# Three partial products of split fp32 weights replaced by one plain fp32 product, in a two-layer encoder on one core

## The chip, the core and the metric

The kernel runs on one NeuronCore of a Trainium2 chip. TensorE multiplies, VectorE, ScalarE and GpSimd work element by element, and SyncE issues most DMAs. The metric is the device time of one execution in microseconds (us); less is better. The change may touch anything inside the kernel, as long as the output is the reference's.

## What is computed

Two layers of an encoder over 256 tokens of 1024 float32 values. Cut to what matters:

```
for layer in range(2):
    hn   = rmsnorm(h, mix_norm_pre[layer])
    proj = hn @ w_in[layer]                  # (256,1024) @ (1024,2048): u, q, k, v of 512 columns each
    y    = concat(pool_mixer(u),             # window means of 2, 4, 8, 16 tokens, each @ a 128x128 matrix
                  neighbourhood_attention(q, k, v))   # 16 heads of 32, 4x64 token grid, 4x16 window
    h    = h + rmsnorm(y @ w_out[layer])     # (256,1024) @ (1024,1024)
    hn   = rmsnorm(h, ffn_norm_pre[layer])
    if layer == 0: f = (silu(hn @ w_gate) * (hn @ w_up)) @ w_down     # dense, inner width 4096
    else:          f = top-2-of-8 experts, the same form, inner width 3584 each
    h    = h + rmsnorm(f)
```

All weights are float32: 12 MB per mixing part (w_in and w_out), 48 MB of dense weights, and 336 MB of expert weights, which are all read once.

## The kernel before

**Stages.** The program is straight-line code for each engine, with semaphores. In order: mixing of layer 0, dense layer, mixing of layer 1, routing, eight expert items, a tail. Between the stages stands a norm (`norm_pair`), whose result is transposed on TensorE (`transposes`, L768) into the tokens `hT`. TensorE's order is written out by hand in each function; nothing is planned by the program but the order of experts.

**Weights of the mixing and dense stages.** SyncE loads them in pieces of 2 MB (a "load", `load` at L456) into a ring of `RING` = 3 buffers. A load has two halves. Before TensorE can use a half, ScalarE rounds it to fp32r (`split_to` at L1177, the ACTIVATE at L1189 that writes `w_hi`), and VectorE writes the rest, `w_lo` = weight - `w_hi` (L1424; in the attention stretch in two parts, L1435). The tokens have the same two parts, `hT_hi` and `hT_lo`, and so have the other left operands (`yaT`, `ypT`, `dhid`). `w_hi` and `w_lo` hold `STAGE` = 3 halves. A load goes on once VectorE has split the one that stood in its buffer.

**A product.** One product is a 128x128 stationary block times 256 or 512 columns. `product` (L728) makes it of three fp32r matmuls:

```python
mm(dst, still[0], moving[0], start=start, stop=False)
mm(dst, still[0], moving[1], start=False, stop=False)
return mm(dst, still[1], moving[0], start=False, stop=stop)
```

The first half of a stage goes through `open_half` (L739), which does the same three in another order (L750, L759). The projection of one mixing stage has 8 halves (`fill(f, part)`, two parts of 8 products of 256 columns), 128 products in all; its output projection has 32 products of 512 columns. The dense layer has 512 products of 256 columns (gate, up) and 128 of 512 columns (down).

Other matmuls (the experts, attention, pooling, the transposes and `keep_busy`) take plain float32 operands. A plain float32 matmul of the program stands as two MATMUL records in the trace; an fp32r matmul stands as one.

**Attention.** It goes in 8 groups g. For each: `scores(g)` on TensorE (L818), `add_bias(g)` on VectorE (L1571 and the minimum at L1573), four exponentials on ScalarE (`exps`, L1292), `normalise(g)` on VectorE (a reciprocal at L1579 and four scalings at L1581), `turn(g)` on TensorE (transposes, L827), a copy on ScalarE (`probs_out`, L1300), and after two groups `values` on TensorE (L844). All groups share the bank `pa` for scores. Before, TensorE's loop is this, and VectorE's loop body is `add_bias(g)`, a half split of weights, `normalise(g)`:

```python
for g in range(GROUPS):
    if g < 7:
        scores(g + 1)
    fill(4 + g // 2, g % 2)
    if g == 7:
        values(2)
    turn(g)
    if g in (3, 4):
        values(g - 3)
```

GpSimd writes the attention bias (`build_bias`, L579) and the window means of pooling (`window_delta`, L387); one of the four means is VectorE's. The four products of the pooling matrices are plain float32 (L926), 256 columns each.

**Experts.** The 192 expert weight "units" of 1792 KB go to 12 slots that lie over the buffers of the earlier stages. `load_unit` (L493) waits for whatever held the slot; the first 12 units are loaded during the mixing of layer 1 and the routing, the others when TensorE is done with a slot. TensorE computes in 32-column strips, four side by side (L1077 for gate and up, L1086 for down). The items take 3, 2, 3, 3, 2, 3, 3 and 2 token groups.

Of the kernel before, what the change touches and what calls it, by code (L numbers as in the profile page):

```python
# [6 lines left out]
ACT = mybir.ActivationFunctionType  # L7
AX = mybir.AxisListType
F32 = mybir.dt.float32
F32R = mybir.dt.float32r  # L10
I32 = mybir.dt.int32

P = 128
D = 1024
# [39 lines left out]
RING = 3  # L54
STAGE = 3
# [3 lines left out]
assert 2 * MOE0 % STAGE == 0  # L59
UNIT = FE  # L60
SLOTS = 12
H_SLOT = 10
# [12 lines left out]
FILL_ENGINE = (0, 1, 0, 0, 0, 1, 0, 1)  # L75
FILLS = (FILL_ENGINE.count(0), FILL_ENGINE.count(1))

# [6 lines left out]
SLOT_OF = [n % SLOTS for n in range(N_UNITS - 2)] + [SLOTS - 1, 0]  # L84
# [25 lines left out]
def hybrid_encoder(nc, x, mix_pre, mix_post, ffn_pre, ffn_post, w_in, pool_w, pool_scale, rpb,  # L110
                   w_out, d_gate, d_up, d_down, router, e_gate, e_up, e_down, consts, out):
    with ExitStack() as ctx:
# [19 lines left out]
        addr = {}  # L132
        bias = sb("bias", [P, HEADS * 2 * ROWS * WIN])
# [5 lines left out]
        w_hi = sb("w_hi", [P, STAGE, 8 * C2], F32R)  # L139
        w_lo = sb("w_lo", [P, STAGE, 8 * C2], F32R)  # L140
        uT = sb("uT", [P, 4, S + 2 * POOL_PAD])
        pt23 = sb("pt23", [P, 2, D])
        h = sb("h", [P, NT, D])
        gpost = sb("gpost", [P, D])
        win_b = sb("win_b", [P, S + 2 * POOL_PAD])
# [3 lines left out]
        assert addr["bias"] + 4 * UNIT * H_SLOT <= addr["h"] and addr["win_b"] <= addr["bias"] + 4 * UNIT * (H_SLOT + 1)  # L149
        sb("spare", [P, (addr["bias"] + 4 * UNIT * SLOTS - plan_top[0]) // 4])  # L150
        hs = sb("hs", [P, NT, D])
        hT_hi = sb("hT_hi", [P, DT, S], F32R)
        hT_lo = sb("hT_lo", [P, DT, S], F32R)
# [6 lines left out]
        ypT_lo = sb("ypT_lo", [P, 4, S], F32R)  # L160
# [11 lines left out]
        prob_b = sb("prob_b", [P, 2, 4, ROWS, COLS], over="spare")  # L172
        assert addr["prob_b"] + 4 * 8 * ROWS * COLS <= addr["hs"]
        pt01 = sb("pt01", [P, 2, D], over="hs")
        assert max(4 * RW, 3 * WORDS) <= 4 * 2 * D
        rwords = [sb("rwords_a", [P, RW], over="pt23"), sb("rwords_b", [P, RW], over="ypT_lo")]
        words0 = [sb(f"words0_{k}", [P, 4 * SEEN], over="pt23", skip=WORDS * k) for k in range(3)]
        words0.append(sb("words0_3", [P, 4 * SEEN], over="ypT_lo"))
        junk = sb("junk", [P, NT, D], over="hT_lo")
        win_c = sb("win_c", [P, S + 2 * POOL_PAD], over="qT")  # L180
        win_d = sb("win_d", [P, S + 2 * POOL_PAD], over="qT", skip=2048)
        hT_full = sb("hT_full", [P, DT, S], over="hT_hi")
        lgT = sb("lgT", [P, S], over="poolw", skip=4 * (DT * CAP + TG * DJ))
        ypT_hi = sb("ypT_hi", [P, 4, S], F32R, over="hT_hi")
        yaT_hi = sb("yaT_hi", [P, 4, S], F32R, over="hT_lo")
        yaT_lo = sb("yaT_lo", [P, 4, S], F32R, over="hT_lo", skip=4 * 4 * S)

        dhid_hi = sb("dhid_hi", [P, 4, S], F32R, over="qT")
        dhid_lo = sb("dhid_lo", [P, 4, S], F32R, over="kT")
# [3 lines left out]
        hid = sb("hid", [P, 2, TG, FJ], over="hT_hi")  # L193
        e = hid[:, :, :, :].rearrange("p h s (t r) -> p h s t r", r=Q)
        hidp = sb("hidp", [P, 2, FT, Q], over="hT_hi", skip=4 * 2 * TG * FJ)
# [5 lines left out]
        units = [sb(f"unit{k}", [P, UNIT], over="bias", skip=4 * UNIT * k) for k in range(SLOTS)]  # L201
# [27 lines left out]
        def heads_out(part):  # L229

            b, m0, m1 = ((0, 0, 4), (1, 0, 2), (1, 2, 4))[part]
            views = [a[:, m0:m1, :].rearrange("p e (r c) -> p (e r) c", r=ROWS)[:, :, QC * b:QC * (b + 1)]
                     for a in (yaT_hi, yaT_lo)]
            return views + [token_order(pd[:, b * C4 + m0 * P:b * C4 + m1 * P])]
# [8 lines left out]
        def columns_half(ap, c):  # L243

            return ap.rearrange("p (t n) -> p t n", t=DT)[:, :, c * C2:(c + 1) * C2]

        def halves(seq, rows_first):

            out_ = []
            for c in range(2):  # L250
                n = 2 * seq + c
                src = ring[:, seq % RING, :]
                hi, lo = w_hi[:, n % STAGE, :], w_lo[:, n % STAGE, :]
                if rows_first:
                    out_.append((src[:, c * 8 * C2:(c + 1) * 8 * C2], hi, lo))
                else:
                    out_.append((columns_half(src, c), hi.rearrange("p (t n) -> p t n", t=DT),
                                 lo.rearrange("p (t n) -> p t n", t=DT)))
            return out_

        def rows_first(seq):

            j = seq % (MIX_LOADS + DENSE_LOADS)
            return 4 <= j < MIX_LOADS or (j >= MIX_LOADS and DENSE[j - MIX_LOADS][0] == "down")

# [9 lines left out]
        hi_ready = sem("hi_ready")  # L275
        first_hi = sem("first_hi")
        split_ready = sem("split_ready")
# [11 lines left out]
        bias_part = sem("bias_part")  # L289
        zeros_ready = sem("zeros_ready")  # L290
# [7 lines left out]
        hT_hi_ready = sem("hT_hi_ready")  # L298
        hT_ready = sem("hT_ready")
# [14 lines left out]
        ypT_hi_ready = sem("ypT_hi_ready")  # L314
        ypT_ready = sem("ypT_ready")
        yaT_hi_ready = sem("yaT_hi_ready")
        yaT_ready = sem("yaT_ready")
        rms_post = sem("rms_post")
        gained = sem("gained")
        bank_done = sem("bank_done")  # L320
        sum_ready = sem("sum_ready")
# [49 lines left out]
        def load_rwords(eng, layer, quarter):  # L371
# [3 lines left out]
            if layer:  # L375
                eng.wait_ge(bias_part, 2 * (n - 1))
# [1479 lines left out]
```

## Time and profile before

| what | value |
|---|---|
| median of 3 runs | 1309.68 us (1309.65 to 1310.13) |
| span of the profiled execution, first to last instruction | 1308.4 us (the page lists no other time for it) |
| mean granted TensorE clock | 0.995 of full |
| TensorE busy | 1285.0 us, 98% of the span |
| VectorE, ScalarE, GpSimd busy | 409.0, 286.0, 108.4 us |
| DMA | 443.50 MB, mean 339 GB/s |
| mixing of layer 0, first to last product of tile 0 | 12.5 to 97.9 us |
| dense layer | 110.9 to 374.7 us |
| mixing of layer 1, the same | 382.3 to 464.8 us |
| experts | 489.1 to 1295.0 us |

A busy time is the time in which at least one instruction of an engine runs, so overlapping matmuls count once. The duration of one matmul (279 ns for 256 columns of fp32r) is longer than the step from one start to the next, since matmuls are pipelined: a rate is to be read from starts. The granted clock says how much of TensorE's 2.4 GHz the chip let through in a stretch.

### The profile page before, as it was taken

The numbers are of one execution on the slowest core, as the hardware profiler recorded it, in microseconds if no ns is written. First come the engines' busy times: TensorE is split into PE (matmuls) and PEld (weight loads), VectorE is DVE, ScalarE is ACT, GpSimd is POOL, SyncE is SP. The second block draws the span as 40 slices with busy tenths as digits, with TensorE's granted clock in tenths as the row PEclk, the third lists the DMA queues.
The fourth block names the chain that finished last, engine by engine and source line by source line (L and its number), as shares of the span: only waits on it lengthen the run. The fifth ranks groups of instructions, "written<-read, shape, count | busy, mean of one in ns | idle before, by whom it ended". The sixth has DMA issues, their size and how long they took to land.

```text
span 1308.4 us, 31062 instructions
## 1 busy us (share of the span) xinstructions
PE 1285.0 (98%) x14397; PEld 794.5 (61%) x14397; DVE 409.0 (31%) x565; ACT 286.0 (22%) x433; POOL 108.4 (8%) x240
## 2 busy tenths in 40 slices
PE   9999999999999999999999999999999999999996
PEld 8888999999989863354353364345353355336443
DVE  6886555555567850030210120030030031021011
ACT  4666344444466630000000000000000000000101
POOL 3334200000000307300000000000000000000000
PEclk9999999999999989999999999999999999999999
DMA  9646855555543399999999999999999999999994
GB/s 303 221 175 211 259 193 193 193 193 193 193 158 141 146 425 427 425 421 398 427 424 426 426 424 425 425 425 425 425 424 425 425 426 424 425 426 424 426 425 187
DMA packets 67012, 443.50 MB, mean 339 GB/s; under 512 B 4520, under 2 KB 10800, under 8 KB 42304
## 3 DMA queue, kind: packets, MB, share of 16 engines
q1 hardware_dynamic: 64736, 433.58, 81.4%
q0 software_dynamic: 2144, 7.90, 2.1%
q8 instruction: 115, 1.88, 0.6%
q14 instruction: 17, 0.14, 0.0%
HBM read 439.36 MB, written 2.10 MB: 337 GB/s over the span
## 4 chain that ended last, share of the span: by engine, by line
PE 90%; DMA 4%; DVE 2%; ACT 1%; SPq 1%; issue 1%; ACTq 0%; DVEq 0%
PE psum L1077 38%; PE psum L1086 18%; PE psum L730 9%; PE psum L732 9%; PE psum L731 9%; DMA unit<-in_moe_w_down 3%; PE psum L1021 2%; PE psum L1032 1%; PE psum L827 1%; DMA ring<-in_w_in 1%; PE psum L818 1%; SPq L385 1%; PE psum L844 1%; ACT pt L1230 1%; PE psum L759 1%
## 5 line engine op out<-in xcount | busy, mean ns | idle before, releaser
L1077 PE MATMUL psum<-unit,xT 128*32 128x448 f32 x5376 | 507.0, 539 | 0.1
L1077 PEld LDWEIGHTS psum<-unit,xT 128*32 128x32 f32 x5376 | 174.9, 110 | 326.9 <-issue 324.8
L1086 PE MATMUL psum<-unit,hid 128*32 128x256 f32 x4704 | 259.1, 380 | 2.4 <-DMA unit<-in_moe_w_down 2.4
L1086 PEld LDWEIGHTS psum<-unit,hid 128*32 128x32 f32 x4704 | 152.0, 110 | 107.0 <-issue 5.3
L1744 DVE TENSOR_TENSOR hidp<-hid,psum 128x448 f32<-128x448 f32 x42 | 38.4, 915 | 535.4 <-PE psum L1077 535.4
L1424 DVE TENSOR_TENSOR w_lo<-ring,w_hi 128x2048 fp32r<-128x2048 f32 x64 | 149.9, 2350 | 112.8 <-ACT w_hi L1189 112.5
L730 PE MATMUL psum<-hT_hi,w_hi 128*128 128x256 f32 x656 | 183.3, 279 | 0.1
L732 PE MATMUL psum<-hT_hi,w_lo 128*128 128x256 f32 x656 | 182.1, 278 | 0.0
L731 PE MATMUL psum<-hT_lo,w_hi 128*128 128x256 f32 x656 | 182.1, 278 | 0.0
L1189 ACT ACTIVATE w_hi<-ring 128x2048 fp32r<-128x2048 f32 x71 | 135.1, 1910 | 59.2 <-PE psum L732 53.0
L730 PEld LDWEIGHTS psum<-hT_hi,w_hi 128*128 128x128 f32 x656 | 123.2, 188 | 2.0 <-issue 1.4
L731 PEld LDWEIGHTS psum<-hT_lo,w_hi 128*128 128x128 f32 x656 | 123.8, 189 | 0.3
L732 PEld LDWEIGHTS psum<-hT_hi,w_lo 128*128 128x128 f32 x656 | 123.2, 188 | 0.0
L1364 ACT ACTIVATE spread<-psum 128x768 f32<-128x768 f32 (+1 forms) x8 | 5.8, 730 | 399.0 <-PE psum L1064 399.0
L1376 ACT ACTIVATE hid<-psum 128x448 f32<-128x448 f32 x42 | 22.8, 543 | 221.2 <-PE psum L1077 220.8
L1724 DVE TENSOR_TENSOR facc<-facc,psum 128x512 f32<-128x512 f32 x28 | 17.4, 683 | 112.4 <-PE psum L1032 112.4
L732 PE MATMUL psum<-w_hi,dhid_lo 128*128 128x512 f32 x128 | 50.5, 395 | 0.0
L731 PE MATMUL psum<-w_lo,dhid_hi 128*128 128x512 f32 x128 | 50.3, 393 | 0.0
L730 PE MATMUL psum<-w_hi,dhid_hi 128*128 128x512 f32 x128 | 49.9, 390 | 0.0
L1382 ACT ACTIVATE y<-psum 128x512 f32<-128x512 f32 x8 | 4.8, 597 | 155.3 <-PE psum L1086 155.3
L1749 DVE STREAM_TRANSPOSE hid<-hidp 128x448 f32<-128x448 f32 x42 | 27.1, 645 | 1.9
L731 PEld LDWEIGHTS psum<-w_lo,dhid_hi 128*128 128x128 f32 x128 | 24.1, 188 | 5.3
(253 smaller groups left out, 947.9 us busy)
## 6 DMA issues: line engine op xcount, KB each, us to landing
unit<-in_moe_w_gate SPq DMA_DIRECT2D x64, 1792.0 KB, 31.8
unit<-in_moe_w_up SPq DMA_DIRECT2D x64, 1792.0 KB, 26.3
unit<-in_moe_w_down SPq DMA_DIRECT2D x64, 1792.0 KB, 31.2
ring<-in_dense_w_gate SPq DMA_DIRECT2D x8, 2048.0 KB, 9.1
ring<-in_dense_w_up SPq DMA_DIRECT2D x8, 2048.0 KB, 9.0
ring<-in_dense_w_down SPq DMA_DIRECT2D x8, 2048.0 KB, 8.2
ring<-in_w_in SPq DMA_DIRECT2D x6, 2048.0 KB, 8.7
ring<-in_w_out SPq DMA_DIRECT2D x4, 2048.0 KB, 8.8
```

The costliest lines, as they stand in the source:

```text
L730: mm(dst, still[0], moving[0], start=start, stop=False)
L731: mm(dst, still[0], moving[1], start=False, stop=False)
L732: return mm(dst, still[1], moving[0], start=False, stop=stop)
L1021: ins = mm(gather_out[s][quad(j)], pick[:, t, Q * s:Q * (s + 1)], blocks, start=t == 0, stop=t == NT - 1)
L1077: ins = mm(bank(half, s)[quad(j)], xT[:, s, dt, :], w[:, at:at + FJ], start=dt == 0, stop=dt == DT - 1)
L1086: ins = mm(down_out[s][quad(j)], e[:, half, s, t, :], w, start=half == t == 0 and s != 2, stop=half == 1 and t == FT - 1, skip_group_check ...
L1189: act.activation(hi, src, ACT.Copy).then_inc(hi_ready, 1)
L1376: act.activation(hid[:, half, s, :], bank(half, s), ACT.Silu).then_inc(silu_done, bank_step(s, groups))
L1424: dve.tensor_tensor(lo, src, hi.bitcast(F32), ALU.subtract).then_inc(split_ready, 1)
L1724: ins = dve.tensor_tensor(part, part, outs[j].rearrange("p (t n) -> p t n", t=NT), ALU.add)
L1744: dve.tensor_tensor(buf.rearrange("p t r -> p r t"), hid[:, half, s, :].rearrange("p (r t) -> p r t", t=FT), bank(half, s).rearrange("p (r ...
L1749: dve.transpose(hid[:, half, s, :], buf.rearrange("p t r -> p (t r)")).then_inc(e_ready, bank_step(s, groups))
```

## The change

`product` becomes a single plain float32 matmul whose operands are the ring buffer itself and the unsplit tokens. All splits on ScalarE and VectorE go (71 ACTIVATEs at L1189, 64 and 16 subtractions at L1424 and L1435), and with them `w_hi`, `w_lo`, `split_to`, `split_part` and `open_half`; the left operands are copied from PSUM once instead of twice. The ring gets a fourth buffer, and a load now waits for TensorE to be done with the buffer (`half_done`). Three expert units go to a buffer of their own (`early`) during the dense layer, and the other nine of the first twelve are issued by other rules. In attention, the halves of the projection are computed in another order (`FILL_ORDER`), other engines copy them out, and TensorE's and VectorE's order is new; on VectorE `normalise(g - 1)` now stands behind `add_bias(g)`. In layer 0 VectorE writes half of the bias. The experts' code is unchanged.

```diff
-RING = 3
-STAGE = 3
+RING = 4
+EARLY_UNITS = (6, 12, 18)
-H_SLOT = 10
+H_SLOT = 11
-FILL_ENGINE = (0, 1, 0, 0, 0, 1, 0, 1)
+FILL_ORDER = (0, 2, 1, 3, 4, 5, 6, 7)
+FILL_ENGINE = (0, 0, 1, 1, 1, 0, 0, 1)
...
             def load(seq, src, tiles):
                 if seq >= RING:
-                    sp.wait_ge(split_ready, 2 * (seq - RING) + 2)
+                    sp.wait_ge(half_done, halves_done(seq - RING))
...
+            load_part(0, 0, part_of(0, 0), half_landed[0])
+            load_rwords(sp, 0, 0)
+            sp.dma_start(cst[:, P:K_ALL], consts[:, P:K_ALL]).then_inc(cst_landed, 16)
+            load_part(1, 0, part_of(0, 1), half_landed[1])
+            load_rwords(sp, 0, 1)
+            load_part(0, 1, part_of(0, 0), w_landed[0])
+            load_part(1, 1, part_of(0, 1), w_landed[1])
+            load_rwords(sp, 0, 2)
+            load_rwords(sp, 0, 3)
+            load_mixing(0, 2)
+            for j, (what, b) in enumerate(DENSE):
...
+                if j in EARLY_UNITS:
+                    load_unit(0, zeroth, EARLY_UNITS.index(j))
+            load_mixing(1, 0)
             sp.wait_ge(scored, GROUPS * DEPTH)
-            load_unit(0, zeroth, 0)
-            sp.wait_ge(delta_dve_ready, DEPTH)
-            load_unit(0, zeroth, 1)
+            load_unit(0, zeroth, 3)
+            load_unit(0, zeroth, 4)
             sp.wait_ge(pv_done, GROUPS * DEPTH)
             sp.wait_ge(delta_ready, 3 * DEPTH)
...
             def product(dst, still, moving, start, stop):
 
-                mm(dst, still[0], moving[0], start=start, stop=False)
-                mm(dst, still[0], moving[1], start=False, stop=False)
-                return mm(dst, still[1], moving[0], start=False, stop=stop)
+                return mm(dst, still, moving, start=start, stop=stop)
...
                 def fill(f, part):
...
                     for dt in range(DT):
-                        tok = (hT_hi[:, dt, :], hT_lo[:, dt, :])
+                        if place == part == 0:
+                            tokens_ready(2 * layer, dt)
                         if f in (4, 5):
...
+                            ins = product(dst, hT[:, dt, part * P:(part + 1) * P], w[:, dt, :], dt == 0, dt == DT - 1)
                         else:
...
+                            ins = product(dst, w[:, dt, part * P:(part + 1) * P], hT[:, dt, :], dt == 0, dt == DT - 1)
...
+                whole(0)
+                whole(2)
+                fill(1, 0)
+                scores(0)
+                fill(1, 1)
+                fill(3, 0)
+                scores(1)
+                fill(3, 1)
...
+                turn(0)
+                fill(4, 0)
+                scores(2)
+                fill(4, 1)
+                turn(1)
+                fill(5, 0)
+                scores(3)
+                fill(5, 1)
+                turn(2)
+                values(0)
+                fill(6, 0)
+                scores(4)
+                turn(3)
+                fill(6, 1)
+                scores(5)
+                turn(4)
+                values(1)
+                fill(7, 0)
+                scores(6)
+                turn(5)
+                fill(7, 1)
+                scores(7)
+                turn(6)
+                values(2)
+                turn(7)
...
@@ vector, mixing
+                    first_bias(0)
+                fill(2, kT[:, 0:2, :])
+                if layer == 0:
+                    first_bias(1)
+                add_bias(0)
+                fill(3, kT[:, 2:4, :])
+                if layer == 0:
+                    first_bias(2)
+                    first_bias(3)
+                add_bias(1)
+                normalise(0)
+                for g in range(2, GROUPS):
+                    if g == 3:
+                        fill(4, vv[:, :, 0:C2])
+                    if g == 7:
+                        fill(7, uT[:, 2:4, POOL_PAD:POOL_PAD + S])
                     add_bias(g)
-                    split_part(h0 + 5 + g // 2, g % 2)
-                    normalise(g)
+                    normalise(g - 1)
+                normalise(7)
```

Two places show how the order of instructions moves. The first is TensorE in the attention of either layer, from the transposes of group 4 on. Rows name line, operation, output and inputs, shape and count; `prob` and `prob_b` are the probabilities of the groups 0 to 3 and 4 to 7. Before, three matmuls make each product of a fill, and 24 of them (8 products) stand between the scores L818 and the next turn L827; three rows of the 24:

```order
L827 MATMUL psum<-cst,prob_b 128x128 x8
L844 MATMUL psum<-pt_58,vv 32x128 x16
L818 MATMUL psum<-kT,qT 128x160 x4
L730 MATMUL psum<-hT_hi,w_hi 128x256
L731 MATMUL psum<-hT_lo,w_hi 128x256
L732 MATMUL psum<-hT_hi,w_lo 128x256
```

The same stretch of the changed kernel, with the groups 4, 5 and 6:

```order
L717 MATMUL psum<-hT,ring 128x256 x8
L789 MATMUL psum<-kT,qT 128x160 x4
L798 MATMUL psum<-cst,prob_b 128x128 x8
L815 MATMUL psum<-pt_57,vv 32x128 x16
L717 MATMUL psum<-hT,ring 128x256 x8
L789 MATMUL psum<-kT,qT 128x160 x4
L798 MATMUL psum<-cst,prob_b 128x128 x8
L717 MATMUL psum<-hT,ring 128x256 x8
L789 MATMUL psum<-kT,qT 128x160 x4
L798 MATMUL psum<-cst,prob_b 128x128 x8
```

The fill that stood between scores and turn has moved ahead of the scores, so that the turn (L798) of group g - 1 follows the scores (L789) of group g directly.

The second place is VectorE in the same stretch. Before, for group 4:

```order
L1571 TENSOR_TENSOR prob_b<-psum,bias 128x16x40
L1573 TENSOR_REDUCE negmax<-prob_b 128x4
L1435 TENSOR_TENSOR w_lo<-ring,w_hi 128x1024
L1579 RECIPROCAL rinv<-sums 128x4
L1581 TENSOR_SCALAR prob_b<-prob_b,rinv 128x4x40 x4
```

In the changed kernel, for the scores of groups 4 and 5 and the scalings of groups 3 and 4:

```order
L1461 TENSOR_TENSOR prob_b<-psum,bias 128x16x40
L1463 TENSOR_REDUCE negmax<-prob_b 128x4
L1469 RECIPROCAL rinv<-sums 128x4
L1471 TENSOR_SCALAR prob<-prob,rinv 128x4x40 x4
L1461 TENSOR_TENSOR prob_b<-psum,bias 128x16x40
L1463 TENSOR_REDUCE negmax<-prob_b 128x4
L1469 RECIPROCAL rinv<-sums 128x4
L1471 TENSOR_SCALAR prob_b<-prob_b,rinv 128x4x40 x4
```

The subtraction of the weights is gone, and the scalings (L1471) behind the scores of group g are those of group g - 1.

## Rows read from the trace of the kernel before

**Rows 1.** The page: busy time of each engine, share of the span, instructions
```profile
PE 1285.0 (98%) x14397; PEld 794.5 (61%) x14397; DVE 409.0 (31%) x565; ACT 286.0 (22%) x433; POOL 108.4 (8%) x240
```

**Rows 2.** Windows by stage: mixing 0, dense, mixing 1, experts; columns in the first line
```profile
core 0: us, PE busy (x) PEld busy (x) DVE busy (x) ACT busy (x) POOL busy (x), PEclk, DMA share, GB/s
...
12.48:97.94 85.46, 82.63 (x721) 74.76 (x722) 67.55 (x97) 52.86 (x103) 31.99 (x28) 1.00 0.68 225
110.90:374.65 263.75, 263.73 (x1920) 247.80 (x1921) 139.21 (x91) 114.54 (x94) 22.77 (x23) 1.00 0.60 206
382.30:464.77 82.47, 82.47 (x721) 75.26 (x722) 57.37 (x93) 50.39 (x100) 10.30 (x16) 1.00 0.47 180
489.10:1294.95 805.85, 803.41 (x10726) 357.80 (x10726) 100.12 (x189) 34.21 (x62) 36.76 (x160) 1.00 1.00 420
```

**Rows 3.** Groups by line: the two splits; busy, mean ns, idle before
```profile
L1424 DVE TENSOR_TENSOR w_lo<-ring,w_hi 128x2048 fp32r<-128x2048 f32 x64 | 149.9, 2350 | 112.8 <-ACT w_hi L1189 112.5
L1189 ACT ACTIVATE w_hi<-ring 128x2048 fp32r<-128x2048 f32 x71 | 135.1, 1910 | 59.2 <-PE psum L732 53.0 <-DMA ring<-in_w_in 6.2
```

**Rows 4.** Timeline, TensorE: start, us, instruction; 256 columns, 96 steps; 512 columns, 27
```profile
199.79 0.28 PE L730 MATMUL psum<-hT_hi,w_hi 128*128 128x256 f32 x1
...
210.67 0.39 PE L730 MATMUL psum<-w_hi,dhid_hi 128*128 128x512 f32 x1
...
463.66 0.40 PE L732 MATMUL psum<-w_hi,ypT_lo 128*128 128x512 f32 x1
...
469.84 0.40 PE L732 MATMUL psum<-w_hi,ypT_lo 128*128 128x512 f32 x1
```

**Rows 5.** Timeline, TensorE: plain float32 products of 128x128 by 256 columns
```profile
85.01 1.89 PE L926 MATMUL psum<-delta,poolw 128*128 128x256 f32 x8
...
471.17 4.05 PE L766 MATMUL psum<-cst 128*128 128x256 f32 x18
```

**Rows 6.** The chain that ended last: start, us, what; the gate and up of item 3
```profile
792.83 72.16 PE psum L1077 x768
```

**Rows 7.** Timeline, mixing 1: VectorE and ScalarE in group 0, VectorE in group 7
```profile
403.21 0.82 DVE L1571 TENSOR_TENSOR prob<-psum,bias 128x640 f32<-128x640 f32 x1 [4.15 <-PE psum L818]
404.07 0.82 DVE L1573 TENSOR_REDUCE negmax<-prob 128x4 f32<-128x640 f32 x1
404.81 1.22 DVE L1435 TENSOR_TENSOR w_lo<-ring,w_hi 128x1024 fp32r<-128x1024 f32 x1
406.72 0.18 DVE L1579 RECIPROCAL rinv<-sums 128x4 f32<-128x4 f32 x1 [0.69 <-ACT prob L1292]
406.93 0.95 DVE L1581 TENSOR_SCALAR prob<-prob,rinv 128x160 f32<-128x160 f32 x4
...
440.33 1.70 DVE L1581 TENSOR_SCALAR prob_b<-prob_b,rinv 128x160 f32<-128x160 f32 x4
...
444.86 0.68 DVE L1558 COPY uT<-psum 128x512 f32<-128x512 f32 x1
```

**Rows 8.** The chain, mixing 1: scores, first matmul of the fill, turn
```profile
410.68 0.74 PE psum L818 x8
411.42 0.32 PE psum L730
414.44 0.87 PE psum L827 x8
```

**Rows 9.** Groups by line: TensorE's waits in the experts' down products
```profile
L1086 PE MATMUL psum<-unit,hid 128*32 128x256 f32 x4704 | 259.1, 380 | 2.4 <-DMA unit<-in_moe_w_down 2.4
```

**Rows 10.** Windows in the routing, columns as above
```profile
477.00:480.00 3.00, 1.93 (x21) 0.87 (x20) 1.43 (x4) 1.29 (x2) 0.00 (x0) 1.00 0.99 413
480.00:483.00 3.00, 1.55 (x10) 1.46 (x14) 2.02 (x11) 0.00 (x0) 0.00 (x0) 0.56 1.05 447
483.00:486.00 3.00, 3.00 (x32) 1.39 (x36) 1.34 (x9) 1.50 (x2) 0.00 (x0) 0.50 0.98 419
486.00:489.00 3.00, 3.00 (x34) 1.82 (x26) 1.05 (x3) 0.00 (x0) 0.00 (x0) 0.80 1.04 440
```

More of the change, by code:

```diff
@@ L200, in hybrid_encoder @@
         spread = sb("spread", [P, NT, TG, P], over="gpre")
-        units = [sb(f"unit{k}", [P, UNIT], over="bias", skip=4 * UNIT * k) for k in range(SLOTS)]
+        units = [sb(f"unit{k}", [P, UNIT], over="early", skip=4 * UNIT * k) for k in range(SLOTS)]
         ident = cst[:, K_ID:K_ID + P]
@@ L241, in pt, with by_columns, by_rows, halves_done @@
             return t[:, k % 2, :].rearrange("p (k m q) -> p k m q", k=2, m=4)
[L243 to L264, printed above, removed]
+        def by_columns(seq, c):
+            return ring[:, seq % RING, :].rearrange("p (t n) -> p t n", t=DT)[:, :, c * C2:(c + 1) * C2]
+        def by_rows(seq, c):
+            return ring[:, seq % RING, c * 8 * C2:(c + 1) * 8 * C2].rearrange("p (t n) -> p t n", t=2)
+        def halves_done(seq):
+            at = seq - mixing_first_load(seq // (MIX_LOADS + DENSE_LOADS))
+            if at < 4:
+                return 2 * (seq - at) + max(FILL_PLACE[2 * at], FILL_PLACE[2 * at + 1]) + 1
+            return 2 * seq + 2
         psum = ctx.enter_context(nc.psum_tensor("psum", [P, 8 * C4], F32))
@@ L482, in _, with load_mixing @@
+            def load_mixing(layer, first):
+                s0, wo = mixing_first_load(layer), by_tile(w_out[layer])
+                for j in range(first, 4):
+                    load(s0 + j, part_of(layer, j), DT)
                 load(s0 + 4, wo[:, 4:8, :], 4)
                 load(s0 + 5, wo[:, 0:4, :], 4)
-                if layer == 0:
-                    for j, (what, b) in enumerate(DENSE):
-                        cut = slice(b * C4, (b + 1) * C4)
-                        if what == "down":
-                            load(MIX_LOADS + j, by_tile(d_down[0, cut]), 4)
-                        else:
-                            w = d_gate if what == "gate" else d_up
-                            load(MIX_LOADS + j, by_tile(w[0])[:, :, cut], DT)
@@ L1259, in norm_pair @@
                     root_of_sums(pre).then_inc(rms_pre, 1)
-                for t in range(NT):
-                    for k in range(1 - t, 2 if n < 2 else 1):
-                        tokens_hi(n + 1, t, k)
+                tokens_low(n + 1, 1)
             def last_norm(value):
@@ L1410, in _ @@
         def _(dve):
-            counts = {"step": 0, "split": 0}
+            counts = {"step": 0}
             def link(ins):
```

494 lines of the change are left out of this document (167 added, 327 removed).

## The prediction

> **What bounds the kernel now.** I read the busy times first: TensorE works 98% of the span, VectorE 31%, ScalarE 22% [rows 1]. Then the windows by stage [rows 2], the reader comparing each stage's length with its PE column: the dense stage is 263.75 us long with TensorE busy for 263.73, mixing 1 is 82.47 with 82.47, mixing 0 is 85.46 with 82.63, the experts 805.85 with 803.41. DMA moves 180 to 225 GB/s in the first three and 420 in the experts, so it has room until the experts start. Then the splits, to see whether they feed TensorE too slowly [rows 3]: a half costs VectorE 2.35 us and ScalarE 1.91, while TensorE spends 16 products of 0.34 us on it, 5.4 us. So TensorE's own work sets the end in every stage; the engines that the change relieves are not waited for. What counts is what one product costs TensorE.
>
> **The product.** Rates come from starts. In [rows 4] 96 steps take 10.88 us, 0.1133 us for an fp32r matmul of 256 columns; 27 steps of 512 columns take 6.18, 0.2289 each. Three of them make a product: 0.340 and 0.687 us. The new product is plain float32. The pooling products and the keep-busy products are just that, 128x128 by 256 columns [rows 5]: 8 records end after 1.89 us, 18 after 4.05. The last one's tail is in both, so ten records cost 2.16 us, 0.216 each. Two records make a product: 0.432 us, or 0.092 more than three fp32r matmuls.
>
> No plain product of 512 columns stands in the trace. Twice the one of 256 is 0.864. From the other side, the experts' gate and up run strips of 448 columns, four side by side: 768 records in 72.16 us [rows 6], 0.094 each, 0.376 for four; scaled to 512 that is 0.430, and 0.859 a product. I take 0.862, 0.175 above the three. The ends differ by 1 us over all 192 products.
>
> The Trainium skill ("TensorE: Matmul & The Clock Gate", section on 56 ns against 53.3 ns) puts the step of a warm matmul at N / 2.4 GHz and 2.5 ns. By that the fp32r steps would be 109.2 and 215.8 ns, less than the 113.3 and 228.9 of the trace, and the whole step from splits to plain would cost 120 us instead of the 104 below. The trace decides: fp32r runs slower than this rule says.
>
> Over the kernel: the dense stage has 512 products of 256 columns and 128 of 512, 512 x 0.092 + 128 x 0.175 = 69.5 us. A mixing stage has 128 and 32: 11.8 + 5.6 = 17.4 us, twice 34.8. Together **+104.3 us**, all on the path, as nothing else fills these stages.
>
> **What the removed work gives.** Splits and second copies of tokens go from ScalarE and VectorE. They were hidden under TensorE [rows 2, 3], except in mixing 0, where TensorE stood still for 85.46 - 82.63 = 2.8 us, and at its first product, which now needs no rounding first: I give 0.5. The ring can't be late: a load is now used for 32 x 0.432 = 13.8 us, and 2 MB take 5 us at 420 GB/s [rows 2]. The norms between stages are as long as before (their chain through VectorE and ScalarE starts with the same last products). **-3.3 us.**
>
> **The attention order.** Here a new wait arises. Before, 24 matmuls of a fill stood between `scores(g + 1)` and `turn(g)`, and in the chain turn follows 3.0 us after the fill's start without a wait [rows 8]. VectorE scaled group g before it touched group g + 1. Now `turn(3)` to `turn(6)` stand directly behind `scores(g + 1)`, and on VectorE `normalise(g)` stands behind `add_bias(g + 1)`, which needs those very scores. So TensorE waits for bias 0.82, start of the minimum 0.04 later, 0.82, reciprocal 0.2, scalings 0.95 [rows 7], and about 0.2 for handing over: 3.0 us. Behind this wait stand the turn, the next fill and all that follows; nobody else can use TensorE. When GpSimd works on the window means the four scalings take 1.70 instead of 0.95 [rows 7]; that meets `turn(4)`, `turn(6)` and, by 0.8 in all, `turn(7)`. Sum: 3.0 + 3.8 + 3.0 + 3.8 + 0.8 = 14.4 us.
>
> `turn(0)` waits as well. VectorE copies the half of fill 3 (0.68 us [rows 7]) before `add_bias(1)` and `normalise(0)`, and fill 3 ends just ahead of `turn(0)`: 0.68 + 0.82 + 0.86 + 0.2 + 0.95 + 0.3 = 3.8 us. In layer 0 two bias steps of the size of one `add_bias` go in between, 5.5 us. `turn(1)` and `turn(2)` have a fill part of 8 x 0.432 = 3.5 us ahead of them, enough cover for 3.0. The later waits (pooling, `values`, the heads) have 3.4 us tiles of projection in front of them and cost nothing. So the waits are 14.4 + 5.5 = 19.9 us in layer 0 and 18.2 in layer 1: **+38.1 us**. From below they can't be negative; the least I allow is half, 19 us, if the other engines hand over faster or the fill's tail hides a part; the most is a third more, 51.
>
> **Early units.** Loading three units in the dense layer, where DMA has room, leaves nine for mixing 1 and the routing, and the last, slot 11, comes with the logits. From there 180 units of 1.835 MB need 786 us at 420 GB/s against TensorE's 803 us of work [rows 2]. TensorE stays the bound and can win no more than the waits it has now: 2.4 us for down units [rows 9] and a little around them. **-3.0 us.**
>
> Sum: 104.3 + 38.1 - 3.3 - 3.0 = +136.1. The profiled span of 1308.4 becomes 1444.5; the median of the runs stood 1.3 us above the span, so the median should be **1446 us**. 0.2% (2.6 us) is about what a measurement of this kernel can tell from no change.
>
> **Rivals.**
>
> *The clock falls in the new waits.* In the routing TensorE was busy for 1.93 of 3 us, then the granted clock was 0.56, 0.50 and 0.80 in the next three windows of 3 us [rows 10]: half rate, 1.2 GHz, for most of 7 us, although TensorE was working again. That loses 3 x (0.44 + 0.50 + 0.20) = 3.4 us. The changed attention has ten waits of 3 us or more. If each let the clock fall, 34 us come on top: 1480; if half did, 1463. For it: the waits are as long as the thin stretch in [rows 10]. Against it: between them stand full matmuls of 5 us, and mixing 0 kept clock 1.00 with its present gaps [rows 2]. The Trainium skill (same page, "What's actually happening") says that throttled is the default and that activity lifts it; this trace agrees with both directions.
>
> *The waits are covered.* If `normalise` is done by the time of `turn`, or TensorE pulls later fills ahead, the 38 us vanish: 1408. Against it: the order of the program, in which VectorE's scalings stand behind a step that needs the scores just issued, and TensorE is in order.
>
> *Faster.* The plain product may be cheap in this place: if one record ran at the fp32r step, products would cost 0.227 and 0.458 us, 768 x 0.113 + 192 x 0.229 = 131 us less than now; with the waits and the rest 1309.7 - 131 + 32 = 1211 us. The point from which it decides: before, products cost 768 x 0.340 + 192 x 0.687 = 393 us; the new ones must cost less than 361, which is 0.157 us a record of 256 columns. Both places with such records show 0.216 [rows 5], and the experts the same rate per column [rows 6]. So little speaks for it.
>
> **How the numbers follow.** The forecast with its own spread (waits of 28 to 48 us, products within 2 us) gets 0.67, 1434 to 1458. The clock gets 0.17, 1458 to 1480. Covered or mostly covered waits get 0.12, 1405 to 1434. The faster case gets 0.02; 0.02 is left for something above 1480 or for no visible change. The range takes the forecast, the lower half of the clock case and the upper half of the covered case: 1424 to 1468. Faster 0.02, within 0.2% 0.01, slower 0.97.
>
> **What the profile will show.** MATMUL records of the ring at 0.216 us from start to start for 256 columns and about 0.430 for 512; a dense stage of 332 us (263.75 + 69.5, perhaps 1.5 less, since the old stage held that much in small gaps); TensorE idle in front of the turns 0, 3, 4, 5 and 6 of each layer, released by VectorE's scalings; mixing stages of about 118 us; an expert stage of 803 us without DMA waits; no change in the tail. A dense stage under 300 us makes the product price wrong; turns without idle time make the wait term wrong; a granted clock of half in attention makes the first rival right.

## The result, and the profile after

The changed kernel takes 1456.8 us (median of 4 runs, 1454.5 to 1459.5) against 1309.7 before: ratio 1.112, 95% interval 1.110 to 1.114, so 147 us slower. The profiled execution has a span of 1456.8 us, 148.4 above that of before.

The page's first section and its rows of slices, to be held against [rows 1]:

```profile
span 1456.8 us, 28896 instructions
...
PE 1403.9 (96%) x13437; PEld 797.7 (55%) x13437; DVE 219.9 (15%) x453; ACT 140.7 (10%) x338; POOL 90.2 (6%) x236
...
PEclk9989999999999998999999999999999999999999
```

VectorE and ScalarE lost about half of their work and the span grew by 148 us. TensorE's share went from 98% to 96%: a new idle time. And the clock row has two dents (an 8 in the third slice, 73 to 109 us, and one in the sixteenth, 546 to 583 us: the attention of each layer).

Stage windows of the changed kernel, from the first product to the transposes behind the stage, then the experts to TensorE's last product (columns as in [rows 2]):

```profile
11.63:143.60 131.97, 114.23 (x584) 83.88 (x585) 37.45 (x86) 33.19 (x98) 18.73 (x24) 0.91 0.46 154
150.48:481.44 330.96, 330.96 (x1281) 243.24 (x1282) 17.02 (x29) 15.92 (x30) 19.17 (x25) 1.00 0.51 176
488.31:617.56 129.25, 113.14 (x584) 83.30 (x585) 34.53 (x81) 33.18 (x98) 10.78 (x18) 0.92 0.32 120
...
636.35:1444.04 807.69, 803.78 (x10726) 356.63 (x10726) 100.29 (x189) 34.21 (x62) 36.74 (x160) 1.00 0.99 414
```

The same three stages of the kernel before, by the same ends (those of [rows 2] stop some products earlier in the two mixing stages):

```profile
12.48:103.23 90.75, 87.92 (x744) 78.95 (x745) 71.20 (x105) 56.10 (x112) 31.99 (x28) 1.00 0.66 219
110.92:374.65 263.73, 263.73 (x1920) 247.78 (x1921) 139.19 (x91) 114.52 (x94) 22.75 (x23) 1.00 0.60 206
382.30:470.07 87.77, 87.77 (x744) 79.45 (x745) 61.03 (x101) 53.63 (x110) 10.93 (x17) 1.00 0.50 195
```

So mixing 0 grew by 41.2 us, the dense stage by 67.2, mixing 1 by 41.5. The start is 0.9 us earlier, the two norms are together 1.6 shorter, the routing 0.2, and everything from the experts' start on is 1.2 longer: 148.4 in all. In the dense stage TensorE is busy without a gap at clock 1.00, so its 67 us are the price of the product. In each mixing stage TensorE is idle for 16 to 18 us, and the clock is 0.91 and 0.92. Where this sits shows in the timeline of mixing 1 (TensorE: start, us, instruction, idle time before it and who ended it):

```profile
513.59 0.81 PE L789 MATMUL psum<-kT,qT 32*128 32x160 f32 x8
514.33 3.72 PE L717 MATMUL psum<-hT,ring 128*128 128x256 f32 x16
521.48 1.09 PE L798 MATMUL psum<-cst,prob 128*128 128x128 f32 x8 [3.43 <-DVE prob L1471]
522.41 5.30 PE L717 MATMUL psum<-ring,hT 128*128 128x256 f32 x16
...
546.30 0.81 PE L789 MATMUL psum<-kT,qT 32*128 32x160 f32 x8
550.02 1.97 PE L798 MATMUL psum<-cst,prob 128*128 128x128 f32 x8 [2.91 <-DVE prob L1471]
551.78 4.34 PE L717 MATMUL psum<-hT,ring 128*128 128x256 f32 x16
556.06 0.81 PE L789 MATMUL psum<-kT,qT 32*128 32x160 f32 x8
560.61 1.97 PE L798 MATMUL psum<-cst,prob_b 128*128 128x128 f32 x8 [3.74 <-DVE prob_b L1471]
```

All five turns wait for VectorE's scalings: 3.43, 2.91, 3.74, 2.91 and 3.12 us for the groups 0 and 3 to 6, 16.1 in all; in layer 0 they are 4.99, 2.94, 3.77, 2.91 and 3.12, 17.7. And the reader should look at the durations behind a wait. The same turn that takes 1.04 us elsewhere (1.09 when it has waited) takes 1.97, the same fill part of 16 records takes 5.30 or 4.34 instead of 3.62. That is TensorE at half clock. The windows say so too (columns as above):

```profile
518.00:522.00 4.00, 0.57 (x6) 0.52 (x6) 3.27 (x8) 1.60 (x8) 0.00 (x0) 1.00 0.63 215
522.00:526.00 4.00, 4.00 (x15) 3.29 (x14) 0.00 (x0) 1.18 (x3) 0.00 (x0) 0.57 0.76 312
526.00:530.00 4.00, 4.00 (x23) 3.17 (x23) 1.39 (x2) 0.00 (x0) 0.00 (x0) 1.00 0.01 2
546.00:550.00 4.00, 1.11 (x10) 0.57 (x8) 2.67 (x7) 1.06 (x5) 0.00 (x0) 0.98 0.00 0
550.00:554.00 4.00, 3.98 (x15) 3.62 (x16) 0.00 (x0) 1.72 (x5) 0.00 (x0) 0.59 0.00 0
```

In a window in which TensorE is nearly idle the clock is still 1.00; in the next, where it works again, it is 0.57. By adding up what each instruction behind a wait takes above its usual time (1.7 us for the fill at 522.41, 0.9 for each doubled turn, and so on), the fallen clock costs about 9 us in mixing 1 and 10 in mixing 0. It differs from execution to execution: the two of the changed kernel with a mean granted clock of 0.980 took 1458.6 (the profiled one) and 1459.5 us, those with 0.983 and 0.985 took 1455.0 and 1454.5.

The theory after this reading (**A**): 148 us are about 97 for the product (67 in the dense stage, the rest in mixing, where 2.8 us of old waits have gone), 34 of waits in front of turns, and 19 of work at a fallen clock behind them. The rivals are written in the expectations below.

### The profile page after: what moved, and what is told of

The parts are those of the page before. It is cut to its first block, busy times and chain, and to the rows that moved or that the text cites. A ratio compares the mean times of both kernels' runs of the same rounds, so it can differ in the third digit from the quotient of the medians.

```text
span 1456.8 us, 28896 instructions
## 1 busy us (share of the span) xinstructions
PE 1403.9 (96%) x13437; PEld 797.7 (55%) x13437; DVE 219.9 (15%) x453; ACT 140.7 (10%) x338; POOL 90.2 (6%) x236
## 4 chain that ended last, share of the span: by engine, by line
PE 93%; DVE 3%; DMA 3%; ACT 1%; issue 0%; DVEq 0%; ACTq 0%; SPq 0%
PE psum L717 35%; PE psum L1050 34%; PE psum L1059 16%; DMA unit<-in_moe_w_down 3%; PE psum L798 2%; PE psum L994 1%; PE psum L1005 1%; PE psum L789 1%; PE psum L815 1%; PE psum L736 1%; DVE negmax L1463 1%; DVE prob_b L1471 1%; DVE prob_b L1461 0%; PE psum L1037 0%; PE psum L748 0%
## 5 line engine op out<-in xcount | busy, mean ns | idle before, releaser
L717 PE MATMUL psum<-hT,ring 128*128 128x256 f32 x1408 | 314.5, 385 | 0.4 <-ACT hT L1176 0.2
L717 PEld LDWEIGHTS psum<-hT,ring 128*128 128x128 f32 x1408 | 271.0, 193 | 42.8 <-issue 5.9
L717 PE MATMUL psum<-ring,dhid 128*128 128x512 f32 x256 | 111.2, 592 | 0.0
L717 PEld LDWEIGHTS psum<-ring,dhid 128*128 128x128 f32 x256 | 48.6, 190 | 57.8 <-issue 57.4
L1605 DVE TENSOR_TENSOR facc<-facc,psum 128x512 f32<-128x512 f32 x28 | 17.4, 681 | 112.2 <-PE psum L1005 112.2
L717 PE MATMUL psum<-ring,hT 128*128 128x256 f32 x128 | 32.7, 414 | 0.0
L798 PE MATMUL psum<-cst,prob_b 128*128 128x128 f32 x64 | 13.2, 374 | 19.6 <-DVE prob_b L1471 19.6
L717 PE MATMUL psum<-ring,yaT 128*128 128x512 f32 x64 | 28.9, 599 | 0.0
L717 PEld LDWEIGHTS psum<-ring,hT 128*128 128x128 f32 x128 | 26.2, 210 | 4.6 <-issue 0.7
L717 PE MATMUL psum<-ring,ypT 128*128 128x512 f32 x64 | 27.8, 592 | 0.0
L798 PE MATMUL psum<-cst,prob 128*128 128x128 f32 x64 | 11.1, 331 | 14.3 <-DVE prob L1471 14.3
L994 PE MATMUL psum<-hs,pick 128*32 128x256 f32 x336 | 22.2, 415 | 1.0 <-DVE pick L1550 1.0
```

What stands on the lines that cost most here:

```text
L717: return mm(dst, still, moving, start=start, stop=stop)
L798: ins = pe.transpose(pb[:, kt * C4 + m * P:kt * C4 + (m + 1) * P], probs(g)[:, m, 2 * kt:2 * kt + 2, :].rearrange("p i j -> p (i j)"), ident)
L994: ins = mm(gather_out[s][quad(j)], pick[:, t, Q * s:Q * (s + 1)], blocks, start=t == 0, stop=t == NT - 1)
L1605: ins = dve.tensor_tensor(part, part, outs[j].rearrange("p (t n) -> p t n", t=NT), ALU.add)
```

## The experiments

### The turns covered by a fill

```diff
                 values(0)
-                fill(6, 0)
                 scores(4)
+                fill(6, 0)
                 turn(3)
-                fill(6, 1)
                 scores(5)
+                fill(6, 1)
                 turn(4)
                 values(1)
-                fill(7, 0)
                 scores(6)
+                fill(7, 0)
                 turn(5)
-                fill(7, 1)
                 scores(7)
+                fill(7, 1)
                 turn(6)
@@ vector
                 add_bias(0)
-                fill(3, kT[:, 2:4, :])
-                if layer == 0:
-                    first_bias(2)
-                    first_bias(3)
                 add_bias(1)
                 normalise(0)
+                fill(3, kT[:, 2:4, :])
+                if layer == 0:
+                    first_bias(2)
+                    first_bias(3)
                 for g in range(2, GROUPS):
...
-                    if g == 7:
-                        fill(7, uT[:, 2:4, POOL_PAD:POOL_PAD + S])
                     add_bias(g)
                     normalise(g - 1)
+                fill(7, uT[:, 2:4, POOL_PAD:POOL_PAD + S])
```

> The changed kernel with another attention order alone: on TensorE each scores(g+1) stands ahead of the fill part and turn(g) behind it, also for the groups 3 to 6, and on VectorE the copies of fill 3 and fill 7 stand behind the scalings. Theory A (the slowdown is the product's price of about 102 us, plus waits of 33.8 us in front of the turns 0, 3, 4, 5 and 6 of both layers, plus about 19.5 us of work at a fallen clock behind these waits): both attention terms go, 1456.8 - 53 = 1403 us, granted clock 1.00 in both mixing stages, no idle time over 0.5 us in front of a turn. Rival B (the turns wait for ScalarE's exponentials or copies, which the order on TensorE does not touch): the waits return in front of other instructions, over 1440 us.

Measured: 1405.4 us (1404.2 to 1406.9), ratio 1.074 (1.072 to 1.076); span 1403.7. Its three stages:

```profile
11.48:115.77 104.29, 103.49 (x584) 76.49 (x585) 37.64 (x86) 32.97 (x98) 19.09 (x24) 1.00 0.58 195
122.65:453.60 330.95, 330.95 (x1280) 243.23 (x1281) 17.03 (x29) 15.92 (x30) 19.19 (x25) 1.00 0.51 176
460.49:564.79 104.30, 103.50 (x585) 76.50 (x586) 34.60 (x81) 32.96 (x98) 11.10 (x17) 1.00 0.39 149
```

The mixing stages lose 27.7 and 25.0 us, the dense stage is the same to 0.01 us, and the clock is 1.00. The expectation holds: 53 us of the slowdown (51 by the medians) come from where the turns stand on TensorE, and two copies on VectorE. The waits did not return elsewhere; only 0.8 us a stage are left, in front of `turn(7)`, where 0.5 had been allowed. Rival B falls. What is left, 95 us above the kernel before, is neither these waits nor the clock.

### Work in the waits, but the waits kept

```diff
                 def turn(g):
+                    if g in (0, 3, 4, 5, 6):
+                        keep_busy(pd[:, C4:2 * C4], ident, cst[:, 0:S], 6 if g else 10 - 3 * layer)
                     pe.wait_ge(prob_ready, GROUPS * layer + g + 1)
```

> The changed kernel with keep-busy products (plain float32, 256 columns, 0.432 us each) put in front of the turns that wait: 6 for groups 3 to 6, 10 and 7 for group 0 of layers 0 and 1; they write a part of PSUM that nobody reads. They fit inside the waits. Theory A: the waits stay as long as they are, but TensorE has work in them and the clock stays at 1.00 in the mixing stages; only the 19.5 us of the fallen clock go, 1437 us. Rival C (the clock in attention is low for another reason than idleness, such as the load of the plain products): clock unchanged at about 0.91, 1457 us or more.

Measured: 1439.8 us (1439.2 to 1441.0), ratio 1.100 (1.099 to 1.102). Mixing 0 as a whole, and a stretch of it:

```profile
11.42:133.43 122.01, 119.64 (x653) 88.65 (x654) 37.59 (x86) 33.18 (x98) 18.75 (x24) 1.00 0.50 167
```

```profile
73.87 3.62 PE L717 MATMUL psum<-hT,ring 128*128 128x256 f32 x16
77.42 0.81 PE L789 MATMUL psum<-kT,qT 32*128 32x160 f32 x8
78.17 2.86 PE L736 MATMUL psum<-cst 128*128 128x256 f32 x12
82.00 1.09 PE L800 MATMUL psum<-cst,prob_b 128*128 128x128 f32 x8 [0.98 <-DVE prob_b L1473]
```

The turn starts 3.8 us behind its scores' end, as it did in the changed kernel, but now takes 1.09 us, not 1.97, and the fill ahead of the scores takes 3.62. Mixing 0 is 122.0 us, which is 10.0 less than in the changed kernel (the clock) and 17.7 more than with covered turns (the waits, of which 17.7 were added up above). Mixing 1 is 120.5 us, 8.8 less than in the changed kernel. Useless products made the kernel 17 us faster, where 19.5 were expected. Rival C falls: with more plain products the clock was 1.00, so it was the idle time that went with the low clock.

### The product alone, in the kernel before

```diff
             def product(dst, still, moving, start, stop):
-                mm(dst, still[0], moving[0], start=start, stop=False)
-                mm(dst, still[0], moving[1], start=False, stop=False)
-                return mm(dst, still[1], moving[0], start=False, stop=stop)
+                return mm(dst, still[0].bitcast(F32), moving[0].bitcast(F32), start=start, stop=stop)
```

> The kernel before with its product as one plain float32 matmul of the rounded parts w_hi and hT_hi alone; splits, order, ring and buffers are those of before, and open_half still makes three fp32r matmuls. The lower parts take no part in the result. 720 products of 256 columns and 192 of 512 change. Theory A: 720 x 0.092 + 192 x 0.175 = 99.9 us on top of 1309.7, 1410 us, nearly all of it in the three stages, granted clock 1.00, no new waits. Rival D (a good part of the slowdown comes from reading operands straight from the ring while DMA writes there, or from the new ring and buffers): clearly less than half of that here, under 1360 us.

Measured: 1403.2 us (1403.1 to 1405.3), ratio 1.073 (1.071 to 1.075). Its stages:

```profile
12.46:115.53 103.07, 102.78 (x601) 76.23 (x601) 71.42 (x107) 56.54 (x112) 30.59 (x28) 1.00 0.59 193
123.02:452.61 329.59, 329.59 (x1296) 242.72 (x1297) 142.30 (x93) 114.14 (x94) 24.17 (x23) 1.00 0.48 164
460.05:562.25 102.20, 102.20 (x601) 76.06 (x602) 62.65 (x103) 54.12 (x110) 10.90 (x17) 1.00 0.48 185
```

The kernel leaves out the lower parts, so it is a measure of time only. The growth over before is 12.3, 65.9 and 14.4 us, with splits still running and the old order, ring and buffers. That is 7 us less than expected for the products. 2.5 of it are the old waits in mixing 0, which shrink from 2.8 to 0.3. Most of the rest lies in the kernel before: over its dense stage the starts of all 1920 matmuls are 0.1143 us apart for 256 columns and 0.2295 for 512 (nearly all single steps 0.112 to 0.119 and 0.225 to 0.234), not 0.1133 and 0.2289 as in the two stretches that the prediction sampled. So the old product had cost more than assumed.

The changed kernel with covered turns is 2.2 us slower than this one by the medians, although it makes 48 more plain products (`open_half` still makes three fp32r matmuls here), 4.4 us at 0.092 each. In the dense stage the two agree: the 329.59 us here and 16 x 0.092 make 331.06, and covered turns took 330.95. Rival D falls: operands read from the ring cost nothing there, and the ring, the fourth buffer and 190 us less work for VectorE are together worth some 2 us of the kernel, about what the medians can tell.

### A fourth pass in the kernel before

```diff
                 mm(dst, still[0], moving[1], start=False, stop=False)
+                mm(dst, still[1], moving[1], start=False, stop=False)
                 return mm(dst, still[1], moving[0], start=False, stop=stop)
```

> The kernel before with a fourth fp32r matmul in product (lower part times lower part). 720 x 0.1133 + 192 x 0.2289 = 125.5 us more work for TensorE. Theory A (TensorE's work is the whole bound of these stages): 1435 us, so that even four split passes cost more than the one plain product of 1410 us. Rival E (the stages are partly bound by splits and DMA, TensorE has slack between halves): well under 1420 us.

Measured: 1437.3 us (1436.9 to 1437.8), ratio 1.099 (1.097 to 1.100), a span of 1435.0 and so 126.6 above before for 125.5 us of counted work. Its dense stage:

```profile
128.30:482.14 353.84, 353.84 (x2545) 331.98 (x2545) 142.36 (x93) 114.43 (x94) 24.27 (x23) 1.00 0.45 154
```

The dense stage took 353.8 us, mixing 108.3 and 107.4. That the sum comes out so close is in part luck: mixing 0 grew by 17.6 us for 20.0 counted, since its old waits took in 2.6, and the dense stage by 90.1 for 85.5, since its matmuls start 0.1158 and 0.2314 us apart, further than before. Apart from those waits no stage had slack that took in the added work, so TensorE's work bounds these stages. Rival E falls.

Four fp32r matmuls cost more here than one plain product (0.463 against 0.432 us for 256 columns). One record of the plain product starts 0.2159 us behind the last, at full clock 518 periods of 2.4 GHz, and 1030 for 512 columns. So, by an estimate from these steps, a record runs through its columns twice and a product four times, with some 6 periods between records; an fp32r matmul, at 0.1143 and 0.2295 us or 274 and 551 periods, runs through them once, with 18 and 39.

### The early units

```diff
-                if j in EARLY_UNITS:
-                    load_unit(0, zeroth, EARLY_UNITS.index(j))
             load_mixing(1, 0)
             sp.wait_ge(scored, GROUPS * DEPTH)
+            for u in range(3):
+                load_unit(0, zeroth, u)
```

> The changed kernel with the three expert units 0 to 2 issued after the mixing loads of layer 1 and the last scores, with the units 3 and 4, instead of during the dense layer. DMA moved only 120 GB/s in mixing 1 and the first 12 units must be there only when the experts start. Theory A (the experts' stage is held by TensorE and by the 12 slots, not by how early the first units came): within 2 us of the changed kernel, 1457 us. Rival F (the early units are worth their transfer time): 3 x 4.3 = 13 us slower, 1470 us.

Measured: 1458.5 us (1457.4 to 1458.8), ratio 1.114 (1.112 to 1.116); the changed kernel beside it (the last run below) 1457.9, 1.112 (1.110 to 1.115). No difference that can be told. The units are issued from 580 us on instead of at 193, 275 and 358, and the experts start at 635.9. Rival F falls.

### Keep-busy products in the routing, in both kernels

In front of the waits of the routing stand 2, 3 and 3 keep-busy products:

```diff
+                keep_busy(pc, ident, cst[:, 0:S], 2)
                 pe.wait_ge(lgT_ready, 1)
...
+                keep_busy(pc, ident, cst[:, 0:S], 3)
                 pe.wait_ge(sel0_ready, 1)
...
+                keep_busy(pc, ident, cst[:, 0:S], 3)
                 gather(0, TG)
```

> The changed kernel with 2, 3 and 3 keep-busy products in front of the waits of the routing, so that the clock does not fall before the gather. The gather took 5.35 us at half clock; at full clock it should take about 3, less some 0.8 us by which the products overshoot the waits: the experts start about 1.5 us earlier. In the changed kernel DMA had no free slot at that time (58 to 196 GB/s in the first 8 us of the stage), so it can follow. Theory G (there TensorE sets the end of the experts' stage): 1.5 us faster than the changed kernel. Rival H (DMA sets the end also there): no gain.

> The same keep-busy products in the kernel before. There DMA runs at 420 GB/s from 460 us on without a pause until its last unit lands, and the last products wait for it. Theory G: the experts start 1.5 us earlier, but the end stays, since DMA's last unit lands when it did: 1309 us, no change beyond 0.5 us. Rival: 1.5 us faster, TensorE being the bound.

> The changed kernel itself, unaltered, on the same chip as the runs beside it: 1457 us, between 1454 and 1460 as its earlier runs.

Measured: in the changed kernel 1457.1 us (1456.1 to 1457.7) beside 1457.9 of the unaltered one (1452.4 to 1458.9): the gain of 0.8 us is inside the spread, the times decide nothing. In the kernel before 1309.4 us, ratio 1.000 (0.999 to 1.001): no change, as expected. The profiles say more. In the kernel before the gather fell from 4.90 to 2.80 us and the experts started 2.95 us earlier, at 486.17. The end did not follow in full (timeline of TensorE in the last item, first of the kernel before, then of it with the keep-busy products):

```profile
1274.22 3.66 PE L1086 MATMUL psum<-unit,hid 128*32 128x256 f32 x64 [0.78 <-DMA unit<-in_moe_w_down]
1278.45 2.80 PE L1086 MATMUL psum<-unit,hid 128*32 128x256 f32 x48 [0.56 <-DMA unit<-in_moe_w_down]
1291.27 3.66 PE L1086 MATMUL psum<-unit,hid 128*32 128x256 f32 x64 [1.06 <-DMA unit<-in_moe_w_down]
```

```profile
1272.82 3.66 PE L1089 MATMUL psum<-unit,hid 128*32 128x256 f32 x64 [1.48 <-DMA unit<-in_moe_w_down]
1277.13 2.80 PE L1089 MATMUL psum<-unit,hid 128*32 128x256 f32 x48 [0.65 <-DMA unit<-in_moe_w_down]
1289.92 3.66 PE L1089 MATMUL psum<-unit,hid 128*32 128x256 f32 x64 [1.03 <-DMA unit<-in_moe_w_down]
```

The waits for DMA grew from 2.4 to 3.8 us in sum, and of 2.95 us 1.35 arrived at the last product. In the changed kernel the same waits are 3.8 us in all three profiles, with the experts starting at 636.35, 634.77 (unaltered, again) and 633.87 (with keep-busy), and the last products at 1440.33, 1438.60 and 1437.59: from the start to this last group of products it is 804 us wherever the stage starts, and 802.2 in the kernel before. So in the changed kernel the end follows the start, as theory G has it. The windows below are its first two items, then the first item of the kernel before with keep-busy products; in the first item of the kernel before itself DMA moved 418 GB/s:

```profile
636.35:747.65 111.30, 111.30 (x1482) 48.53 (x1486) 12.17 (x26) 4.07 (x7) 36.74 (x160) 1.00 0.96 381
747.65:826.12 78.47, 78.47 (x1064) 35.36 (x1060) 10.88 (x22) 3.64 (x7) 0.00 (x0) 1.00 1.00 420
```

```profile
486.17:597.46 111.29, 111.29 (x1482) 48.53 (x1486) 12.11 (x26) 4.08 (x7) 37.00 (x160) 1.00 1.01 422
```

When the experts of the changed kernel start, 11 units have landed and the twelfth follows 3.5 us later, so all slots are taken and DMA pauses until TensorE frees one. The issue and the landing of every unit in the traces (times from the start of the stage) show what becomes of the lead. From the 13th unit on, issues go by freed slots and come at the same times in all these kernels, most to 0.1 us, the last at 766.8. The 21st unit lands at 50.2 us in the changed kernel and at 52.6 in the kernel before. The 37th lands at 125.9 and 124.6, after a stretch in which units were issued only some 9 us ahead of their landing; with keep-busy products in the kernel before, where DMA had no pause, at 125.5. From there on several units are always queued, they land about 4.37 us apart, and the last lands 35 to 37 us after its issue: at 802.1 us in the kernel before, at 803.7 with keep-busy products in it and at 803.9 in the changed kernel. The last product waits for this unit. So it is DMA that ends the stage in all of them, and the lead of the changed kernel is gone after some 126 us. The other profiles agree: 804.2 us with covered turns and 804.2 with the units not early, 803.6 with the plain product in the kernel before. Whether one more slot would move the end was not tried.

No version beat the kernel before: the nearest ones, the plain product alone and the covered turns, are 95 and 97 us slower than the kernel before run beside them, and keep-busy products in its routing change nothing.

## Why the prediction was right, and what it missed

The forecast was 1446 us with a range of 1424 to 1468; measured were 1456.8. Direction and size were right, 136 us forecast of 147, but the sum came so close because terms that failed went both ways: the clock and the experts added nearly 25 us that it did not have, the product and the waits took 10 less. With the other terms as forecast, the clock alone would have given 1466. That 1456.8 lies in the band of 1434 to 1458, given to a clock that does not fall, is luck.

- **The bound.** TensorE's own work bounds every stage, by the prediction. Right for mixing and the dense stage, shown by the fourth pass (every stage grew by about its counted work) and by the plain product alone. For the experts' last item it was wrong, as told below.
- **The product's price.** 104.3 us were forecast, 98.5 measured: 67.2 of 69.5 in the dense stage, and, by the covered turns without their 0.8 us of waiting, 15.6 (the 2.8 us of old waits put back) and 15.7 in the two mixing stages, of 17.4 each. The price of the plain product was right: 0.2167 us a record in the first fills (80 records in 17.50 us), and 0.429 for 512 columns (32 records in 13.90), forecast 0.216 and 0.431. What was mis-sized is the old product. Its 0.340 and 0.687 us came from two short stretches; with the mean steps of the whole dense stage, 0.1143 and 0.2295 us, it takes the 263.7 us of that stage, with 0.1133 and 0.2289 only 262.0. In mixing, where scores, turns and `values` stand between the products, the old ones took 68.5 us a stage instead of 65.5.
- **The waits.** Forecast 38.1, measured 33.8, at the five turns named. The single wait of 3.0 us was 2.9; `turn(4)` with GpSimd active was 3.8, as read from the scalings of 1.70 us [rows 7]. Mis-sized were `turn(0)`, 3.4 and 5.0 instead of 3.8 and 5.5, and `turn(6)`, 3.1 instead of 3.8. There the four scalings took 1.15 us, although GpSimd worked on window means all the while (VectorE and GpSimd in mixing 1, around the scalings ahead of `turn(4)` and `turn(6)`):

```profile
558.78 1.77 DVE L1471 TENSOR_SCALAR prob_b<-prob_b,rinv 128x160 f32<-128x160 f32 x4
558.79 0.64 POOL L389 TENSOR_TENSOR delta<-win_a,uT 128x256 f32<-128x256 f32 x1
559.51 0.73 POOL L381 TENSOR_TENSOR win_a<-uT 128x271 f32<-128x271 f32 x1
...
581.37 1.15 DVE L1471 TENSOR_SCALAR prob_b<-prob_b,rinv 128x160 f32<-128x160 f32 x4
581.73 1.04 POOL L385 TENSOR_SCALAR win_a<-win_a 128x256 f32<-128x256 f32 x1
```

In the slow case GpSimd ran operations on two inputs (TENSOR_TENSOR), in the other mostly its own scaling (TENSOR_SCALAR). `turn(7)` waited for nothing instead of 0.8.
- **The clock.** This is the term that failed. The forecast put it at zero and gave the falling clock a chance of 0.17, with 34 us if every wait let it fall and 17 us if half did. Measured were 19 us by adding up instructions, 20.4 by what the covered turns took away besides the waits. That is near the case of half the falls, but it is not that case: behind each of the ten waits there is work at a lower clock, for 1.3 to 2.9 us of loss each by adding up, and not the 3.4 that the routing gave. The sentence against it, that mixing 0 kept 1.00 with its present gaps, compared gaps of at most 1.3 us with gaps of 3. The longest of mixing 0 in the kernel before:

```profile
42.74 1.09 PE L827 MATMUL psum<-cst,prob 128*128 128x128 f32 x8 [1.29 <-DVE prob L1581]
```

The rows of the routing were the better witness, and the prediction had quoted them.
- **What was given back.** Forecast for the start 0.5, measured 0.9; the two norms gave 1.6 us that the forecast didn't have; the first product no longer waits for all four copies of tokens, which would explain it but was not tried by itself.
- **The experts.** Forecast 3.0 us faster, measured 1.2 slower. The step that failed is the last part of that paragraph: "TensorE stays the bound and can win no more than the waits it has now", with DMA's 786 us for 180 units against TensorE's 803. It counted DMA's time from the start of the stage on and took the 12 slots as a lead that is kept. But for the first 126 us DMA gets units only as slots come free, and the 155 units after that need 678 us, so that the last lands at 804. The waits for DMA grew from 2.4 to 3.8 us.

Added up, clock +20, experts +4, waits -4, product -6, and norms, start and routing -2 make 12 us, for 12.3 between the forecast of +136.1 and the +148.4 of the profiled spans.

## What to carry to other kernels

Where TensorE is the bound, work for idle engines that saves it passes can be free: here splitting weights costs 190 us of VectorE's time and 145 of ScalarE's and saves some 95 us of the kernel's. Before a plain float32 product is put in place of three reduced ones, compare what each costs from start to start, not the number of instructions.

When an order is written by hand, ask of each wait what is queued between the producer's input and the waiting instruction. A step that needs 3 us on other engines wants 3 us of work behind its trigger, and moving the work so that five turns a layer have it behind their trigger was worth 53 us, over a third of it clock. Where such a wait can't be covered, products that nobody reads keep the clock up, provided that they fit inside the wait.

## What the runs showed of the hardware that was not expected

- A wait of 2.9 us in front of a turn was enough for the granted clock to fall to half for the work behind it, 1.97 us instead of 1.04 for the same turn; other waits of the same length (3.12 us at 582.58, turn of 1.09) were followed by full clock at once, and by half only later. The "TensorE: Matmul & The Clock Gate" page of the Trainium skill (section "What's actually happening") has an idle TensorE fall back to 1.2 GHz; the runs agree, and show that the bill comes in the work after the idle time, not in it.
- One fp32r matmul steps at 0.1143 us for 256 columns and 0.2295 for 512 over the dense stage of the kernel before, nearly all single steps of 256 columns from 0.112 to 0.119 us, and at 0.1158 and 0.2314 with a fourth pass; why the steps differ was not tested. One record of a plain float32 product steps at 0.2159 and 0.4292, nearly always to 0.001 us, also with the splits running beside it. Four fp32r passes were therefore 7% dearer than the plain product for 256 columns (0.463 against 0.432 us).
- VectorE's four scalings take 0.94 us with GpSimd quiet. While GpSimd works on two-input operations of the window means they take 1.70 us in the kernel before and 1.77 in the changed one; while it runs mostly its own scaling they take 1.15.
